# Narrow matrix products of a hybrid decoder step placed on different column tiles, two scan steps at a time

## The chip, the core and the metric

The kernel runs on one core of a Trainium2 chip. A core has five engines with instruction streams of their own: TensorE (PE, matrix products into the PSUM banks), VectorE (DVE), ScalarE (ACT), GpSimd (POOL) and SyncE (SP, which here only issues transfers). Engines wait for each other through semaphores. The metric is the device time of one execution in microseconds, a median over several runs.

## The reference, cut to what matters

One inference step of a decoder layer for 512 prompt tokens and 8 sample tokens. After a projection `z = h @ w_in`, three mixers run: a diagonal complex state-space model (SSM), sparse attention with gates per head, and a short convolution. Their merged output goes through `w_out`, and a mixture of experts follows, whose router chooses a group of experts and two experts in it.

```python
    bu_re = jnp.einsum('blgc,gpc->blgp', ug, bbar_re)
    bu_im = jnp.einsum('blgc,gpc->blgp', ug, bbar_im)
    ...
    _, _, hr, hi = lax.associative_scan(complex_affine_combine, (a_r, a_i, bu_re, bu_im), axis=1)
    y = (jnp.einsum('blgp,gcp->blgc', hr, c_re.astype(f32))
         - jnp.einsum('blgp,gcp->blgc', hi, c_im.astype(f32)))
    y = y.reshape(bsz, seq, SSM_DIM) + d_skip.astype(f32) * u32
    ...
    gates = jax.nn.sigmoid(gate_logits.astype(f32)).reshape(bsz, seq, 3, KV_HEADS, grp)[..., None]
    ...
    lg = (t @ w_rg).astype(f32) + b_rg.astype(f32)
    le = ((t @ w_re).astype(f32) + b_re.astype(f32)).reshape(n_tok, N_EXPERT_GROUPS, EXPERTS_PER_GROUP)
```

## The kernel before

Features lie on the partitions and tokens on the free axis, 520 tokens in two halves of 260 (`CHUNKS`). All data are fp32, and each product written in the code appears in the trace as two passes of the same shape.

The order on every engine is written out by hand. The projection is cut into 22 tiles of 128 columns (`z_tile`, L1527). The SSM has 24 groups, scanned two at a time in 12 steps (`SN`), and the steps are interleaved with the tiles. In step i, TensorE does the tiles `beside[i]` (two in steps 0 to 8, one in step 9, none in 10 and 11), then `bu(i + 1)`, the scan's input products (L1539 for the prompt, L1541 for the samples), then `y(i)`, the outputs (L1551 and L1552, real and imaginary part). The 32 output rows of step i go to partitions 32 * (i % 4) of bank 6, so four steps fill the bank. In step 9 the product of the attention gates (24 outputs, L1612, banks 0 and 1) stands before `bu(10)`; in step 10 the prompt's compression comes before y(10), in step 11 the prompt's scores (L1587) before y(11).

VectorE's step i is a chain: angles and coefficients (L1037 to L1044, with the angles of step i + 1 between them), products with bu (L1050 to L1060; after the first of them TensorE may overwrite bu, `v_done`), two hardware scans (L1063, L1066), four products with cosine and sine into `cgr`, `sgr`, `sgi`, `cgi` (L1070 to L1073), and the states `hr` and `hi` (L1076, L1077), which release y(i) through `h_ready`. One pair of buffers holds the states, so L1076 of step i waits for y(i - 1) (`y_done`). After every fourth step VectorE adds the skip term to bank 6 (L1084) and with this frees the bank (`skip_ready`).

ScalarE copies the projection's tiles out of PSUM and computes sine and cosine. GpSimd does the short convolution (from L589) beside the scan, one block of channels as its tiles become ready, and starts most page loads of the cache. In the attention stage `hidden_part` (L1720) compresses cached blocks with weights of 64 columns, key on column tile 0 and value on column tile 64, in turn.

Late in the kernel the output projection (L1857) makes eight tiles; after each one, `logits(n - 1)` multiplies one block of the normalised tokens with the router's 20 columns (L1846), halves of tokens in banks 6 and 7.

Of the kernel before, what the change touches and what calls it, by code (L numbers as in the profile page):

```python
# [11 lines left out]
ACT = mybir.ActivationFunctionType  # L12
# [4 lines left out]
KD = D // P  # L17
# [133 lines left out]
def build(nc, io):  # L151
    ctx = ExitStack()
    with ctx:
# [82 lines left out]
        def cc(name, rows=P):  # L236
# [165 lines left out]
        hr, hi = WORK[:, 10, :], WORK[:, 11, :]  # L402

        pR, pI, qR, qI, vr, vi, gr, gi, cgr, cgi, sgr, sgi = (
            CMP[:, 1, 2048 + 512 * j:2560 + 512 * j] for j in range(12))
        kint = ki.bitcast(I32)
# [313 lines left out]
        def _(act):  # L720
# [25 lines left out]
            for i in range(SN):  # L746
# [7 lines left out]
                if i == 9:  # L754
                    act.wait_ge(z_done, NZ + 1)
                    for c, (a, b) in enumerate(CHUNKS):
                        mm = act.activation(Gt[:, a:b], bank[c][0:24, 0:HALF], ACT.Sigmoid)
                    mm.then_inc(z_ready, 1)
# [155 lines left out]
            act.activation(lgT[:, HALF:T], bank[7][0:20, 0:HALF], ACT.Copy).then_inc(lt_ready, 1)  # L914
# [49 lines left out]
        def _(dve):  # L964
# [67 lines left out]
            for i in range(SN):  # L1032
# [36 lines left out]

                step(dve.tensor_tensor(cgr, c, gr, ALU.mult), 1)  # L1070
# [3 lines left out]
                if i >= 1:  # L1074
                    dve.wait_ge(y_done, i)
# [437 lines left out]
        def _(pe):  # L1513
# [31 lines left out]
            def y(i):  # L1545

                r = slice(32 * (i % 4), 32 * (i % 4) + 32)
                pe.wait_ge(h_ready, i + 1)
                if i >= 4:
                    pe.wait_ge(skip_ready, i // 4)  # L1550
                pe.matmul(bank[6][r, :], CT[:, i, 0, :], hr, start=True, stop=False, tile_position=(0, r.start))  # L1551
                pe.matmul(bank[6][r, :], CT[:, i, 1, :], hi, start=False, stop=True,  # L1552
                          tile_position=(0, r.start)).then_inc(y_done, 1)
# [49 lines left out]
            for i in range(SN):  # L1603
                for t in beside[i]:
                    z_tile(t)
                if i == 9:

                    pe.wait_ge(wg_in, 16)
                    pe.wait_ge(z_ready, NZ - 1)
                    for k in range(KD):  # L1610
                        for c, (a, b) in enumerate(CHUNKS):
                            mm = pe.matmul(bank[c][0:24, 0:HALF],  # L1612
                                           wgt[:, k, :], H[:, k, a:b], start=(k == 0), stop=(k == KD - 1))
                    mm.then_inc(z_done, 1)
# [6 lines left out]
                y(i)  # L1621
# [220 lines left out]
            def logits(k):  # L1842

                pe.wait_ge(norm_ready, KD + k + 1)
                for c, (lo, hi_) in enumerate(CHUNKS):
                    mm = pe.matmul(bank[6 + c][0:20, 0:HALF], rw[:, k, :], H[:, k, lo:hi_], start=(k == 0),  # L1846
                                   stop=(k == KD - 1))
# [255 lines left out]
```

## Time and profile before

| | |
|---|---|
| three runs, us | 1056.26, 1060.02, 1060.38 (median 1060.02) |
| the profiled execution, us | 1054.12, span 1052.4 |
| mean granted TensorE clock | 0.937 of full speed |
| busy, share of the span | PE 90%, DVE 55%, ACT 25%, POOL 25% |
| chain that ended last | PE 59%, DVE 27%, DMA 5%, issue 5%, ACT 2% |
| L1527 (projection tiles) | 704 passes, 159.4 us busy |
| L1551 and L1552 (y) | 24 passes each, 592 ns and more each by the record |

The profile is one execution. Times in its rows are microseconds from the span's start. A record of a matmul includes its way through the array, and neighbouring records overlap, so the cost of one in a dense stretch is the distance from start to start, which the chain of waits shows directly. The chain follows the work that ended last back from the end: an engine's line in it means that this work set the time there. Idle time in brackets in a timeline names who ended it.

### The profile page before, as it was taken

The page shows a single profiled execution, that of the slowest core. Times are in us where ns is not written, and L with a number is a line of the kernel's source. Part 1 is how long each engine was busy: PE and PEld are TensorE (multiplying, and loading weights), DVE is VectorE, ACT ScalarE, POOL GpSimd, SP SyncE. Part 2 cuts the span into 40 slices and gives each one's busy share as a digit, 9 for nine tenths or more (in the row PEclk, how much of TensorE's full clock was granted, in tenths as well). Part 3 has the DMA queues.
Part 4 walks back from the last instruction along what each step waited for, and adds up shares of the span by engine and source line. Part 5 has one row for each costly group of instructions (what it writes and reads, how often), then busy time and mean ns, then how long its engine had stood idle before and what let it go on. Part 6 is the DMA issues. An engine that isn't in the chain of part 4 may idle for free.

```text
span 1052.4 us, 14165 instructions
## 1 busy us (share of the span) xinstructions
PE 942.6 (90%) x4998; PEld 647.9 (62%) x4998; DVE 581.4 (55%) x982; ACT 258.5 (25%) x569; POOL 261.9 (25%) x285
## 2 busy tenths in 40 slices
PE   4999999998698999899999979989973999999934
PEld 3777776754565666688888858867752333333314
DVE  2697699899655777498999970001135121112125
ACT  3111211222446667322112111211140111111102
POOL 3020065500334541012143512220002122222030
PEclk8999999997799999799999989989995999999967
DMA  8333111110547867114322602381121699999563
GB/s 322 123 98 103 41 61 59 61 62 1 165 139 237 267 207 273 58 56 183 121 76 82 236 32 70 93 360 61 60 68 35 215 337 346 339 333 336 194 164 120
DMA packets 57266, 162.97 MB, mean 155 GB/s; under 512 B 14364, under 2 KB 33325, under 8 KB 51957
## 3 DMA queue, kind: packets, MB, share of 16 engines
q1 hardware_dynamic: 41685, 130.39, 35.4%
q0 software_dynamic: 15520, 31.79, 10.2%
q8 instruction: 36, 0.59, 0.2%
q14 instruction: 25, 0.20, 0.1%
HBM read 197.46 MB, written 18.58 MB: 205 GB/s over the span
## 4 chain that ended last, share of the span: by engine, by line
PE 59%; DVE 27%; DMA 5%; issue 5%; ACT 2%; SPq 2%; POOL 1%; DVEq 0%; POOLq 0%; ACTq 0%
PE bank L1932 11%; PE bank L1527 9%; PE bank L1772 6%; PE bank L1857 6%; PE bank L1958 5%; DVE BIG L1213 5%; PE bank L1720 5%; DVE BIG L1209 3%; PE bank L1781 3%; DMA BIG<-in_w_o 2%; PE bank L1665 2%; DVE BIG L1194 2%; DVE WORK L1195 2%; PE bank L1675 2%; PE bank L1686 1%
## 5 line engine op out<-in xcount | busy, mean ns | idle before, releaser
L1772 PE MATMUL bank<-H,BIG 128*128 128x260 f32 x768 | 175.3, 387 | 1.4 <-ACT AUX L869 1.4
L1527 PE MATMUL bank<-H,BIG 128*128 128x260 f32 x704 | 159.4, 388 | 8.0 <-DVE H L716 8.0
L1772 PEld LDWEIGHTS bank<-H,BIG 128*128 128x128 f32 x768 | 147.2, 192 | 25.6 <-issue 1.8
L1527 PEld LDWEIGHTS bank<-H,BIG 128*128 128x128 f32 x704 | 134.4, 192 | 36.5 <-issue 15.9
L1932 PE MATMUL bank<-BIG,H 128*64 (+1 forms) x512 | 114.8, 601 | 1.9 <-issue 1.9
L434 POOL DMA_DIRECT2D BIG<-in_cmp x128 | 69.8, 546 | 128.4 <-issue 95.8
L1932 PEld LDWEIGHTS bank<-BIG,H 128*64 128x64 f32 x512 | 37.1, 139 | 76.0 <-issue 76.0
L1781 PE MATMUL bank<-BIG 128*128 128x260 f32 x320 | 76.1, 390 | 2.1 <-DVEq L1312 1.3
L1720 PE MATMUL bank<-BIG,AUX 128*64 128x256 f32 x512 | 70.7, 398 | 3.5 <-issue 3.5
L1781 PEld LDWEIGHTS bank<-BIG 128*128 128x128 f32 x320 | 62.0, 194 | 12.4 <-DVEq L1312 1.4
L1857 PE MATMUL bank<-WORK,BIG 128*128 128x260 f32 x256 | 60.1, 394 | 5.2 <-DMA BIG<-in_w_o 5.2
L624 POOL TENSOR_TENSOR AUX<-AUX 128x520 f32<-128x520 f32 x16 | 34.8, 2173 | 113.0 <-ACT AUX L875 113.0
L1475 DVE COPY BIG<-bank 128x256 f32<-128x256 f32 x16 | 6.8, 424 | 98.3 <-PE bank L1943 98.3
L1958 PE MATMUL bank<-BIG 128*64 (+1 forms) x256 | 58.5, 598 | 1.6 <-DVE BIG L1475 1.0
L1857 PEld LDWEIGHTS bank<-WORK,BIG 128*128 128x128 f32 x256 | 49.3, 195 | 15.7 <-issue 8.2
L1213 DVE TENSOR_TENSOR BIG<-BIG 128x2048 f32<-128x2048 f32 (+4 forms) x40 | 51.3, 1282 | 1.4
L869 ACT ACTIVATE AUX<-bank 128x260 f32<-128x260 f32 x48 | 16.0, 385 | 130.5 <-PE bank L1772 130.4
L1327 DVE TENSOR_TENSOR BIG<-BIG,bank 128x260 f32<-128x260 f32 x16 | 6.1, 422 | 73.6 <-PE bank L1857 73.6
L1720 PEld LDWEIGHTS bank<-BIG,AUX 128*64 128x64 f32 x512 | 34.2, 141 | 18.9 <-issue 9.9
L622 POOL TENSOR_TENSOR WORK<-AUX 128x520 f32 x8 | 16.1, 2013 | 106.2 <-ACT AUX L875 106.2
L642 POOL DMA_INDIRECT H<-h_rows,token_i x16 | 15.9, 995 | 103.6 <-DVEq L1455 98.8
L1481 DVE TENSOR_SCALAR WORK<-bank,WORK 128x512 f32<-128x512 f32 x16 | 12.0, 751 | 48.1 <-PE bank L1958 48.1
(411 smaller groups left out, 1378.2 us busy)
## 6 DMA issues: line engine op xcount, KB each, us to landing
BIG<-in_w_gu SPq DMA_DIRECT2D x16, 2048.0 KB, 9.2
BIG<-in_cmp POOLq DMA_DIRECT2D x128, 128.0 KB, 3.5
BIG<-in_cmp SPq DMA_DIRECT2D x128, 128.0 KB, 3.4
BIG<-in_w_d SPq DMA_DIRECT2D x16, 1024.0 KB, 8.7
BIG<-in_w_m SPq DMA_DIRECT2D x24, 512.0 KB, 3.5
BIG<-in_w_z SPq DMA_DIRECT2D x22, 512.0 KB, 3.3
y_rows<-WORK SPq DMA_DIRECT2D x16, 512.0 KB, 9.1
o_win<-BIG SPq DMA_DIRECT2D x2, 2048.0 KB, 9.3
```

Source lines behind the costliest of these rows:

```text
L434: engine.dma_start(CMP[:, b, g * 256:g * 256 + 256], io["cmp"][bass.ds(at, 1)].rearrange("o p n -> p (o n)")).then_inc(arrived, 16)
L624: pool.tensor_tensor(SG[:, b], SG[:, b], BB[:, b], ALU.mult).then_inc(pool_step, 1)
L1194: step(dve.tensor_tensor(P3, KV[br][0], QR[:, m].unsqueeze(1).broadcast_to([P, SELB, HD]), ALU.mult))
L1209: step(dve.tensor_tensor(P3, KV[br][1], SE[:, br, m].unsqueeze(2).broadcast_to([P, SELB, HD]), ALU.mult))
L1213: step(dve.tensor_tensor(P3[:, 0:keys], P3[:, 0:keys], P3[:, keys:2 * keys], ALU.add))
L1527: mm = pe.matmul(bank[2 * (t % 2) + c][:, 0:HALF], W_RING[:, t % 2, k, :], H[:, k, a:b], start=(k == 0), stop=(k == KD - 1))
L1720: mm = pe.matmul(bank[6 + b][v * HD:v * HD + HD, 0:2 * NCB], w1[:, v, r, :], page[b][:, :, v, :, r, :].rearrange("p g h c -> p h g c"), st ...
L1772: mm = pe.matmul(bank[c][:, 0:HALF], W_RING[:, b, k, :], H[:, k, lo:hi_], start=(k == 0), stop=(k == KD - 1))
L1781: mm = pe.matmul(bank[2 + c][:, 0:HALF], WB[:, b, k, :], Z[:, y0 + k, lo:hi_], start=(k == 0), stop=(k == nk - 1))
L1857: mm = pe.matmul(bank[2 * b + c][:, 0:HALF], W_RING[:, b, k, :], M[:, k, lo:hi_], start=(k == 0), stop=(k == KD - 1))
L1932: mm = pe.matmul(bank[2 + i % 2][r, :].rearrange("p (w f) -> p w f", w=2), XT[i % 2][:, k * P + r.start:k * P + r.stop], w[:, :, k, :], st ...
L1958: mm = pe.matmul(bank[5 + half][r, :], ACTT[i % 2][:, f * P + r.start:f * P + r.stop], w[:, f, 512 * half:512 * half + 512], start=(f == 0 ...
```

## The change

Three narrow products are placed on other column tiles of TensorE. The outputs of two scan steps, i and i + 1, are computed together after step i + 1's `bu`, in the order real part of i, real part of i + 1, imaginary part of i, imaginary part of i + 1. For this the states need two pairs of buffers: even steps keep the old one, odd steps write them in place into `cgr` and `sgr`. VectorE therefore waits for the outputs before the four products of an even step and no longer before the states. The gates' and the router's second half of tokens goes to output partitions from 64 instead of 0, and the readers on ScalarE follow.

```diff
@@ build
-        hr, hi = WORK[:, 10, :], WORK[:, 11, :]
...
+        states = ((WORK[:, 10, :], WORK[:, 11, :]), (cgr, sgr))
@@ ScalarE: gates' sigmoid, router's logits to SBUF
-                        mm = act.activation(Gt[:, a:b], bank[c][0:24, 0:HALF], ACT.Sigmoid)
+                        mm = act.activation(Gt[:, a:b], bank[c][64 * c:64 * c + 24, 0:HALF], ACT.Sigmoid)
...
-            act.activation(lgT[:, HALF:T], bank[7][0:20, 0:HALF], ACT.Copy).then_inc(lt_ready, 1)
+            act.activation(lgT[:, HALF:T], bank[7][64:84, 0:HALF], ACT.Copy).then_inc(lt_ready, 1)
@@ VectorE: scan step i
+                if i >= 2 and i % 2 == 0:
+                    dve.wait_ge(y_done, i)
                 step(dve.tensor_tensor(cgr, c, gr, ALU.mult), 1)
                 step(dve.tensor_tensor(sgr, s, gr, ALU.mult), 1)
                 step(dve.tensor_tensor(sgi, s, gi, ALU.mult), 1)
                 step(dve.tensor_tensor(cgi, c, gi, ALU.mult), 1)
-                if i >= 1:
-                    dve.wait_ge(y_done, i)
+                hr, hi = states[i % 2]
                 step(dve.tensor_tensor(hr, cgr, sgi, ALU.subtract), 1)
                 step(dve.tensor_tensor(hi, sgr, cgi, ALU.add))
@@ TensorE: outputs of the scan
-            def y(i):
-
-                r = slice(32 * (i % 4), 32 * (i % 4) + 32)
-                pe.wait_ge(h_ready, i + 1)
+            def y_pair(i):
+
+                pe.wait_ge(h_ready, i + 2)
                 if i >= 4:
                     pe.wait_ge(skip_ready, i // 4)
-                pe.matmul(bank[6][r, :], CT[:, i, 0, :], hr, start=True, stop=False, tile_position=(0, r.start))
-                pe.matmul(bank[6][r, :], CT[:, i, 1, :], hi, start=False, stop=True,
-                          tile_position=(0, r.start)).then_inc(y_done, 1)
+                for part in range(2):
+                    for n in (i, i + 1):
+                        r = slice(32 * (n % 4), 32 * (n % 4) + 32)
+                        mm = pe.matmul(bank[6][r, :], CT[:, n, part, :], states[n % 2][part], start=(part == 0),
+                                       stop=(part == 1), tile_position=(0, r.start))
+                        if part:
+                            mm.then_inc(y_done, 1)
@@ TensorE: gates' product
-                            mm = pe.matmul(bank[c][0:24, 0:HALF],
-                                           wgt[:, k, :], H[:, k, a:b], start=(k == 0), stop=(k == KD - 1))
+                            mm = pe.matmul(bank[c][64 * c:64 * c + 24, 0:HALF], wgt[:, k, :], H[:, k, a:b],
+                                           start=(k == 0), stop=(k == KD - 1), tile_position=(0, 64 * c))
@@ TensorE: loop over scan steps
-                y(i)
+                if i % 2:
+                    y_pair(i - 1)
@@ TensorE: logits
-                    mm = pe.matmul(bank[6 + c][0:20, 0:HALF], rw[:, k, :], H[:, k, lo:hi_], start=(k == 0),
-                                   stop=(k == KD - 1))
+                    mm = pe.matmul(bank[6 + c][64 * c:64 * c + 20, 0:HALF], rw[:, k, :], H[:, k, lo:hi_],
+                                   start=(k == 0), stop=(k == KD - 1), tile_position=(0, 64 * c))
```

On TensorE in the scan, before, from the end of bu(1) (L1541) on: each step has its own y behind bu.

```order
L1541 MATMUL bank<-BIG,TWICE 128x8
L1551 MATMUL bank<-WORK,TWICE 32x512
L1552 MATMUL bank<-WORK,TWICE 32x512
L1527 MATMUL bank<-H,BIG 128x260 x32
L1539 MATMUL bank<-BIG,TWICE 128x512
L1541 MATMUL bank<-BIG,TWICE 128x8
L1539 MATMUL bank<-BIG,TWICE 128x512
L1541 MATMUL bank<-BIG,TWICE 128x8
L1551 MATMUL bank<-WORK,TWICE 32x512
L1552 MATMUL bank<-WORK,TWICE 32x512
L1527 MATMUL bank<-H,BIG 128x260 x32
```

The same place after the change (L1528 is the projection's tile, L1540 and L1542 are bu): from bu(1) through the first pair, L1554.

```order
L1542 MATMUL bank<-BIG,TWICE 128x8
L1528 MATMUL bank<-H,BIG 128x260 x32
L1540 MATMUL bank<-BIG,TWICE 128x512
L1542 MATMUL bank<-BIG,TWICE 128x8
L1540 MATMUL bank<-BIG,TWICE 128x512
L1542 MATMUL bank<-BIG,TWICE 128x8
L1554 MATMUL bank<-WORK,TWICE 32x512
L1554 MATMUL bank<-BIG,TWICE 32x512
L1554 MATMUL bank<-WORK,TWICE 32x512
L1554 MATMUL bank<-BIG,TWICE 32x512
L1528 MATMUL bank<-H,BIG 128x260 x32
L1540 MATMUL bank<-BIG,TWICE 128x512
```

Step 0 has no y left; the y of steps 0 and 1 stand behind bu(2), real and imaginary parts in turn, and read WORK (even step) and BIG (odd step).

On TensorE at the end of the scan, before: the prompt's compression (L1558, L1560), y(10), the scores (L1587), y(11), then transposes.

```order
L1558 MATMUL bank<-w,BIG 16x64 x2
L1560 MATMUL bank<-BIG,w 64x16 x2
L1551 MATMUL bank<-WORK,TWICE 32x512
L1552 MATMUL bank<-WORK,TWICE 32x512
L1587 MATMUL bank<-BIG 128x512 x4
L1551 MATMUL bank<-WORK,TWICE 32x512
L1552 MATMUL bank<-WORK,TWICE 32x512
```

After the change (compression L1562 and L1564, scores L1591):

```order
L1562 MATMUL bank<-w,BIG 16x64 x2
L1564 MATMUL bank<-BIG,w 64x16 x2
L1591 MATMUL bank<-BIG 128x512 x4
L1554 MATMUL bank<-WORK,TWICE 32x512
L1554 MATMUL bank<-BIG,TWICE 32x512
L1554 MATMUL bank<-WORK,TWICE 32x512
L1554 MATMUL bank<-BIG,TWICE 32x512
```

The y of step 10 has left its place before the scores and stands with that of step 11 behind them.

On VectorE in step 2, before, from the second scan (L1066) on; names in brackets are the semaphores waited for:

```order
L1066 SCALAR_TENSOR_TENSOR BIG<-spar,BIG 128x512 [waits dve_step]
L1070 TENSOR_TENSOR BIG<-WORK,BIG 128x512 [waits dve_step]
L1071 TENSOR_TENSOR BIG<-WORK,BIG 128x512 [waits dve_step]
L1072 TENSOR_TENSOR BIG<-WORK,BIG 128x512 [waits dve_step]
L1073 TENSOR_TENSOR BIG<-WORK,BIG 128x512 [waits dve_step]
L1076 TENSOR_TENSOR WORK<-BIG 128x512 [waits y_done,dve_step]
L1077 TENSOR_TENSOR WORK<-BIG 128x512 [waits dve_step]
L1079 COPY hlast<-WORK 128x1 [waits dve_step]
```

The same place after the change, where L1072 to L1075 are the four products and L1077, L1078 the states:

```order
L1066 SCALAR_TENSOR_TENSOR BIG<-spar,BIG 128x512 [waits dve_step]
L1072 TENSOR_TENSOR BIG<-WORK,BIG 128x512 [waits dve_step,y_done]
L1073 TENSOR_TENSOR BIG<-WORK,BIG 128x512 [waits dve_step]
L1074 TENSOR_TENSOR BIG<-WORK,BIG 128x512 [waits dve_step]
L1075 TENSOR_TENSOR BIG<-WORK,BIG 128x512 [waits dve_step]
L1077 TENSOR_TENSOR WORK<-BIG 128x512 [waits dve_step]
L1078 TENSOR_TENSOR WORK<-BIG 128x512 [waits dve_step]
L1080 COPY hlast<-WORK 128x1 [waits dve_step]
```

The wait for `y_done` has moved four products up, to the first of an even step; odd steps have none.

## Rows read from the trace of the kernel before

**Rows 1.** Chain of waits, scan step 1: start us, us, engine, tile, line, count.
```profile
69.28 14.22 PE bank L1527 x64
83.50 1.05 PE bank L1539 x2
...
85.75 0.97 PE bank L1551 x2
86.73 0.86 PE bank L1552 x2
```

**Rows 2.** Timeline of DVE, steps 4 to 8: start us, us, line, out<-in [idle before <-releaser].
```profile
124.33 0.75 DVE L1084 SCALAR_TENSOR_TENSOR BIG<-BIG,sdb,bank 128x512 f32<-128x512 f32 x1 [8.59 <-PE bank L1552]
125.22 0.49 DVE L1037 TENSOR_SCALAR WORK<-WORK,spar 128x512 f32<-128x512 f32 x1
...
140.65 0.90 DVE L1037 TENSOR_SCALAR WORK<-WORK,spar 128x512 f32<-128x512 f32 x1
...
159.82 0.68 DVE L1077 TENSOR_TENSOR WORK<-BIG 128x512 f32<-128x512 f32 x1
...
194.44 0.68 DVE L1077 TENSOR_TENSOR WORK<-BIG 128x512 f32<-128x512 f32 x1
...
200.14 0.75 DVE L1084 SCALAR_TENSOR_TENSOR BIG<-BIG,sdb,bank 128x512 f32<-128x512 f32 x1 [4.53 <-PE bank L1552]
201.03 1.41 DVE L1037 TENSOR_SCALAR WORK<-WORK,spar 128x512 f32<-128x512 f32 x1
```

**Rows 3.** Timeline of PE, bu(6) and y(5).
```profile
158.72 0.28 PE L1541 MATMUL bank<-BIG,TWICE 32*128 32x8 f32 x2
160.61 1.04 PE L1551 MATMUL bank<-WORK,TWICE 128*32 128x512 f32 x2 [1.61 <-DVEq L1078]
```

**Rows 4.** Timeline of PE, end of the scan: y(10), scores, y(11), samples' outputs.
```profile
252.52 1.92 PE L1551 MATMUL bank<-WORK,TWICE 128*32 128x512 f32 x2
...
256.07 4.41 PE L1587 MATMUL bank<-BIG 128*128 128x512 f32 x8
261.45 1.04 PE L1551 MATMUL bank<-WORK,TWICE 128*32 128x512 f32 x2 [0.96 <-DVEq L1078]
262.33 1.02 PE L1552 MATMUL bank<-WORK,TWICE 128*32 128x512 f32 x2
...
268.63 0.88 PE L1639 MATMUL bank<-hlast,TWICE 128*32 128x8 f32 x48 [3.46 <-DVEq L1105]
```

**Rows 5.** Chain of waits, output projection and router.
```profile
707.70 9.13 PE bank L1857 x32
...
724.33 0.98 PE bank L1846 x4
725.32 7.21 PE bank L1857 x32
...
765.31 0.98 PE bank L1846 x4
```

**Rows 6.** Timeline of PE, compression of the cached blocks in the attention stage.
```profile
292.38 1.08 PE L1720 MATMUL bank<-BIG,AUX 128*64 128x256 f32 x8
293.30 0.39 PE L1686 MATMUL bank<-WORK 128*64 128x128 f32 x4
```

**Rows 7.** Windows: stretch, length, PE PEld DVE ACT POOL busy, PEclk, DMA, GB/s.
```profile
160.00:180.00 20.00, 18.57 (x77) 13.83 (x78) 19.63 (x28) 2.56 (x7) 11.31 (x10) 1.00 0.17 53
266.00:268.00 2.00, 0.00 (x0) 0.00 (x0) 1.76 (x8) 0.00 (x0) 0.00 (x0) 0.95 0.00 0
268.00:270.00 2.00, 0.88 (x48) 0.81 (x48) 0.80 (x4) 0.00 (x0) 0.50 (x1) 0.50 0.06 11
```

**Rows 8.** Timeline of GpSimd (POOL), third channel block of the convolution.
```profile
192.42 3.84 POOL L589 TENSOR_TENSOR rstd<-BIG 128x520 f32<-128x520 f32 x1 [20.32 <-ACT BIG L728]
```

**Rows 9.** Timeline of PE, the gates' product.
```profile
227.48 7.19 PE L1612 MATMUL bank<-H,wgt 128*24 128x260 f32 x32
```

**Rows 10.** Timeline of DVE, first use of bu(10).
```profile
238.12 0.68 DVE L1050 TENSOR_TENSOR BIG<-WORK,bank 128x512 f32<-128x512 f32 x1
```

## The prediction

> **What bounds the kernel now.** I read the chain of waits through the scan stage first, since most of the diff lies there, then the timelines of TensorE (PE) and VectorE (DVE) where the chain changes engine. In a step with two projection tiles the chain runs on PE alone: 64 passes of the tiles in 14.22 us, two input products (`bu`), then `y` in 0.97 + 0.86 = 1.83 us, and the next tiles at once [rows 1]. The reader should see that nothing lies between these pieces: PE is full, and a microsecond off `y` is a microsecond off the step. DVE meanwhile is done early and waits: 8.59 us before the skip-add of step 3 and 4.53 before that of step 7 [rows 2]. After each skip-add the roles change: steps 4 to 6 and 8 to 11 run at DVE's pace, a step from 125.22 to 140.65 being 15.4 us, and PE waits for h, 1.61 us before y(5) [rows 3], 0.96 before y(11) [rows 4]. So PE time is worth something in steps 0 to 3 and 7, and little elsewhere until step 11, where y(11) is on the path alone. In the output projection (L1857) the chain is PE again: 7.21 us a tile and 0.98 for the router's four passes between two tiles [rows 5].
>
> **What a pair costs.** Every fp32 product is two passes: a 260-column one takes 14.22/64 = 0.222 us, a 512-column one about 0.43 (0.86 for L1552's two) [rows 1]. The trace has no pair of 32-column tiles side by side. It has the like: L1720 alternates two 64-column tiles, two passes on each, and eight passes of 256 columns take 1.08 us, the next line starting after 0.92 [rows 6]. One after the other they would take 8 x 0.219 = 1.75 us (0.222 scaled to 256 columns). Five times 0.219 is 1.09: the second pass of one tile runs beside the first of the other, so eight passes fill five slots. The new pair has the same order (two passes on tile n, two on n+1, and again). I price it at 5 x 0.43 + 0.11 = 2.26 us, the 0.11 being what the first half of y takes over two slots (0.97 - 0.86). Bounds: four slots (1.83) if all overlapped, eight (3.55) if nothing did. The Trainium skill (TensorE: Matmul & The Clock Gate, Part 3: Packing small matmuls) has a rule against this: weight loads overlap matmuls in flight only when the row groups differ, and all tiles here use all rows. By that rule the pair would take the upper bound and no edit here would gain; the 1.08 us of [rows 6], on tiles that share all rows too, disagrees with it.
>
> **Steps 0 to 3.** Four y of 1.83 go (7.32), two pairs come (4.52): the skip-add of step 3 starts 2.8 us earlier, at 121.5 instead of 124.33 [rows 2].
>
> **Steps 4 to 7.** DVE waits for nothing in them and moves with the skip-add, so h(5) is ready at 160.50 - 2.8 = 157.7 and h(7) at 195.12 - 2.8 = 192.3 [rows 2]. PE ends bu(6) at 159.00 [rows 3]; now 2.8 earlier and without y(4), at 154.4. It then waits 3.4 us for h(5): the wait of 1.61 grows, since the pair needs the odd step's h and PE has less to do before it. The pair ends at 160.0. Two rounds of tiles and bu follow, 16.47 each (69.28 to 85.75, [rows 1]), now without y(6) between them; PE reaches the next pair at 192.9, 0.6 after h(7), and ends it at 195.2. The skip-add of step 7 starts at 195.3 against 200.14: 4.8 earlier. PE and DVE meet there almost together, so nothing more is to be had from PE, and any delay of PE after step 5 is paid in full.
>
> **The clock in the new wait.** That delay is likely. Through today's waits of up to 1.61 us the granted clock stays 1.00 (160 to 180 us); in the 3.46 us before the product at 268.63 it falls, 0.95 in 266 to 268 and 0.50 (the 1.2 GHz level) after [rows 4, 7]. The new 3.4 us is as long as that one. A restart at the low level costs what the first output tile after the idle stretch shows: 9.13 us against 7.21, 1.9 us [rows 5]. Bounds are 0 (the clock holds) and 1.9; I take 1.9. What is late next is the pair of steps 6 and 7, and with it the skip-add: 2.9 earlier instead of 4.8.
>
> **GpSimd beside DVE.** GpSimd starts its third convolution at 192.42 [rows 8], and DVE's first operation of step 8 takes 1.41 us where that of step 4 took 0.49 [rows 2]. DVE's idle time from h(7) to the skip-add hides part of this. It was 5.0 us; with the fall of the clock it is still about 4.9 and nothing changes, without it 3.0, and I charge 0.6 (bounds 0 and two operations longer by 0.92).
>
> **Steps 8 to 11.** DVE sets the pace and waits for no product, so y(8), y(9) and the gates' product leave covered time. The gates' 32 passes (7.1 us from 227.48, [rows 9]) become 17 slots, 3.8 us; bu(10) after them is used by DVE at 238.12, without a wait, right behind its own work [rows 10]. Worth 0; without DVE's cover it would be 3.3. The last pair takes the place of y(11): 2.26 against 1.90 (261.45 to 263.35, [rows 4]), about +0.35, if the clock is high. Today y(10) (1.92 for two passes, low clock) and the scores stand before it and bring the clock up, and y(11) starts after 0.96 us idle at full speed [rows 4]. Now y(10) moves into the pair, the scores come sooner, and the waits before h(9) and bu(11) grow by about 2 to 4 us. At the low clock the pair takes 5 x 0.96 = 4.8, +2.9. Between 0.35 and 2.9 I take 1.0, nearer the low end since eight dense passes of the scores still run shortly before it.
>
> **DVE's own edits** cost nothing: the same count of operations of the same shapes, odd steps writing in place. The wait for y_done moves from the end of every step to the four products of even ones. Behind it stand those products and h; the pair it waits for runs right after the bu that the same step uses, and between that use and the four products DVE has ten operations, two of them scans. If it were not, its delay would go into every second step.
>
> **Router.** The logits were already 32-column work at (0,0); moving the second half to column 64 makes 3 slots of 4 passes: 0.22 us a visit. Six of the eight visits lie before the last output tile's end [rows 5]: -1.3. The other two lie beside ScalarE's work, 0. Bounds: 0 and -1.8.
>
> **Sum.** -4.8 + 1.9 + 0 + 1.0 - 1.3 = -3.2 us. The profiled execution took 1054.12 us (span 1052.4), 5.9 under the median of the three runs, 1060.02. I make the forecast against that median: 1056.8; a profiled execution like the one shown would take 1050.9.
>
> **Rivals.**
> 1. The clock holds through the new wait. For it: bu before and the pair after are dense. Against: the 3.46 us row. -4.8 + 0.6 + 0.35 - 1.3 = -5.2, 1054.8.
> 2. A cold tail: the longer waits of steps 9 and 10 leave the clock low until the last pair. For it: the tail is at the low level already when y(10) runs. Against: the scores lie before the pair. The tail term is 2.9 instead of 1.0: 1058.7.
> 3. The other side, and the change not doing what it says: 32-column tiles do not run side by side. With p for a pair, the skip-add of step 7 moves by 4p - 13.9 (two pairs in steps 0 to 3, one in 5, one in 7) and the tail by p - 1.9: 5p - 15.8, zero at p = 3.15, about seven slots of eight. At eight, p = 3.55 gives +1.9 and the router 0: 1061.9, and 1063.8 with the clock's fall. For it: no row shows 32-column tiles at once. Against: the 64-column row. The Trainium skill's rule above would lead here.
>
> **How the numbers follow.** Forecast 0.45, rival 1 0.25, rival 2 0.15, rival 3 0.10, others 0.05. Predicted is the likeliest, 1056.8. The runs shown spread over 4.1 us, so each case carries about 2 us either way; 1052.5 to 1061 takes in the first three and leaves out most of rival 3 and the lower edge of rival 1. Half a per cent, 5.3 us, is about what a measurement can tell from no change. Under 1054.7 lie nearly half of rival 1, a sixth of the forecast and some of the others: 0.27. Over 1065.3 lie only rival 3 with the clock and stray cases: 0.05. Within: 0.68.
>
> **What would show it.** In the changed kernel's timeline: a pair group of eight passes lasting near 2.2 us (3.5 refutes the pricing); skip-adds near 121.5 and 195 to 197; PE idle 3 to 4 us before the pair of steps 4 and 5, with the granted clock at 0.5 there or 1.0 (decides rival 1); the gates' group near 3.8 us with no change in DVE; router visits near 0.76 us. Wrong would be the prediction if DVE waited at its new wait, if the scan's end moved by under 1 or over 6 us, or if time moved after the scan other than at the router.

## The result, and the profile after the change

| | before | after |
|---|---|---|
| median of four runs each, us | 1058.37 (1056.26 to 1060.38) | 1045.72 (1044.50 to 1046.84) |
| ratio, 95% interval | | 0.9883 [0.9854, 0.9913] |
| profiled execution, us (span) | 1054.12 (1052.4) | 1046.84 (1045.2) |
| mean granted TensorE clock | 0.937 | 0.930 |

The change is faster, by more than the forecast and outside its range (1052.5 to 1061). The two profiled executions differ by 7.3 us, the medians by 12.65; that the two numbers differ is itself a finding, taken up below.

In the changed kernel L1528 is the projection's tile, L1540 and L1542 are bu, L1554 is the pair, L1616 the gates, L1591 the scores, L1862 the output projection, L1851 the router, L1085 VectorE's skip-add. The chain of waits through the scan, from bu(2) and the first pair on (start, length, what), answers to [rows 1]:

```profile
81.15 1.05 PE bank L1540 x2
...
83.40 1.84 PE bank L1554 x8
85.24 14.22 PE bank L1528 x64
```

Eight passes of 512 columns take 1.84 us where a single y of four passes took 1.83 [rows 1]. The second state's output is free. The timeline of TensorE shows how, and then the places where the engine waited. A row here is one pass or a run of alike passes, with its start and length; the time in brackets is the wait before it.

```profile
83.33 0.62 PE L1554 MATMUL bank<-WORK,TWICE 128*32 128x512 f32 x1
83.34 0.62 PE L1554 MATMUL bank<-BIG,TWICE 128*32 128x512 f32 x1
83.79 0.59 PE L1554 MATMUL bank<-WORK,TWICE 128*32 128x512 f32 x1
83.79 0.59 PE L1554 MATMUL bank<-BIG,TWICE 128*32 128x512 f32 x1
...
156.45 1.06 PE L1554 MATMUL bank<-WORK,TWICE 128*32 128x512 f32 x1 [3.46 <-DVEq L1079]
...
157.31 1.06 PE L1554 MATMUL bank<-WORK,TWICE 128*32 128x512 f32 x1
...
160.01 14.88 PE L1528 MATMUL bank<-H,BIG 128*128 128x260 f32 x64
...
229.08 1.06 PE L1554 MATMUL bank<-WORK,TWICE 128*32 128x512 f32 x1 [4.05 <-DVEq L1079]
...
236.26 2.02 PE L1540 MATMUL bank<-BIG,TWICE 32*128 32x512 f32 x2 [3.55 <-DVEq L1057]
...
251.19 6.48 PE L1591 MATMUL bank<-BIG 128*128 128x512 f32 x8 [0.84 <-ACT vcp L774]
257.60 0.62 PE L1554 MATMUL bank<-WORK,TWICE 128*32 128x512 f32 x1
```

Read the starts: a pass of the even step (WORK) and one of the odd step (BIG) begin within 0.01 us of each other, and the next two 0.43 us later. So four slots, not five. At 156.45 TensorE has waited 3.46 us, and the passes on one tile now start some 0.85 us apart (157.31) where it was 0.43: the new wait costs the clock, as forecast. The waits ahead of 229.08 and 236.26 are as long, and the work after them is slow too, but the last pair at 257.60 is at full speed. The granted clock (PEclk, the third value from the end) in windows of that stretch, to be held against [rows 7]:

```profile
154.00:156.00 2.00, 0.00 (x0) 0.00 (x0) 2.00 (x4) 0.00 (x0) 1.80 (x3) 0.60 0.00 0
156.00:160.00 4.00, 3.55 (x8) 0.56 (x8) 3.78 (x8) 0.00 (x0) 3.81 (x3) 0.50 0.02 4
160.00:162.00 2.00, 2.00 (x8) 1.71 (x7) 2.00 (x4) 0.00 (x0) 1.92 (x2) 0.69 0.00 0
162.00:164.00 2.00, 2.00 (x11) 1.71 (x10) 2.00 (x5) 0.00 (x0) 1.90 (x2) 1.00 0.00 0
```

VectorE's skip-adds of steps 3, 7 and 11 (start, length, and in brackets its wait), which answer to [rows 2]:

```profile
120.19 0.75 DVE L1085 SCALAR_TENSOR_TENSOR BIG<-BIG,sdb,bank 128x512 f32<-128x512 f32 x1 [6.80 <-PE bank L1554]
...
195.62 0.75 DVE L1085 SCALAR_TENSOR_TENSOR BIG<-BIG,sdb,bank 128x512 f32<-128x512 f32 x1 [4.94 <-PE bank L1554]
...
259.66 0.75 DVE L1085 SCALAR_TENSOR_TENSOR BIG<-BIG,sdb,bank 128x512 f32<-128x512 f32 x1 [2.62 <-PE bank L1554]
```

The third stands in the trace of before at:

```profile
263.46 0.75 DVE L1084 SCALAR_TENSOR_TENSOR BIG<-BIG,sdb,bank 128x512 f32<-128x512 f32 x1 [1.64 <-PE bank L1552]
```

They come 4.1, 4.5 and 3.8 us earlier. The scan hands on 3.8 us. Most of the rest comes from the router, in the chain of waits through the output projection, where a visit takes 0.55 us against 0.98 in [rows 5]:

```profile
720.12 0.55 PE bank L1851 x4
720.67 7.21 PE bank L1862 x32
...
758.93 0.55 PE bank L1851 x4
```

Six such visits lie on the chain, 0.43 us each: 2.6 us. The first tile of the output projection starts 4.3 us earlier (703.41 against 707.70), the end of that stage comes 6.8 us earlier (766.7 against 773.5), the end of the span 7.2.

### The profile page after: what moved, and what is told of

Read it like the earlier page. It is cut to its first block, busy times and chain, and to the rows that moved or that the text cites. A ratio compares the mean times of both kernels' runs of the same rounds, so it can differ in the third digit from the quotient of the medians.

```text
span 1045.2 us, 14150 instructions
## 1 busy us (share of the span) xinstructions
PE 930.3 (89%) x4998; PEld 644.6 (62%) x4998; DVE 580.0 (55%) x982; ACT 258.5 (25%) x569; POOL 267.5 (26%) x285
## 4 chain that ended last, share of the span: by engine, by line
PE 62%; DVE 24%; DMA 5%; issue 4%; ACT 2%; SPq 2%; POOL 1%; DVEq 0%; POOLq 0%; ACTq 0%
PE bank L1937 11%; PE bank L1528 10%; PE bank L1777 6%; PE bank L1862 6%; PE bank L1963 5%; DVE BIG L1214 5%; PE bank L1725 5%; DVE BIG L1210 3%; PE bank L1786 3%; DMA BIG<-in_w_o 2%; PE bank L1670 2%; PE bank L1540 2%; DVE BIG L1195 2%; DVE WORK L1196 2%; PE bank L1680 2%
## 5 line engine op out<-in xcount | busy, mean ns | idle before, releaser
L1528 PE MATMUL bank<-H,BIG 128*128 128x260 f32 x704 | 159.8, 388 | 7.8 <-DVE H L716 7.8
L1528 PEld LDWEIGHTS bank<-H,BIG 128*128 128x128 f32 x704 | 134.7, 193 | 33.1 <-issue 12.4
L1862 PE MATMUL bank<-WORK,BIG 128*128 128x260 f32 x256 | 60.2, 395 | 5.1 <-DMA BIG<-in_w_o 5.1
L1862 PEld LDWEIGHTS bank<-WORK,BIG 128*128 128x128 f32 x256 | 49.4, 195 | 15.7 <-issue 8.1
L622 POOL TENSOR_TENSOR WORK<-AUX 128x520 f32 x8 | 18.8, 2354 | 103.3 <-ACT AUX L875 103.3
```

Source lines behind the costliest of these rows:

```text
L1528: mm = pe.matmul(bank[2 * (t % 2) + c][:, 0:HALF], W_RING[:, t % 2, k, :], H[:, k, a:b], start=(k == 0), stop=(k == KD - 1))
L1862: mm = pe.matmul(bank[2 * b + c][:, 0:HALF], W_RING[:, b, k, :], M[:, k, lo:hi_], start=(k == 0), stop=(k == KD - 1))
```

## The experiments

Twelve kernels ran in three sets, each set beside the kernel before on the same chip. Ratios are to the kernel before of the same set, with 95% intervals.

**Both kernels again, and the change in parts.** The kernel before and the changed kernel unchanged; then only the pairs (the gates' and the router's second half back at partition 0); then only the router; in the second set only the gates. ScalarE's readers of the moved halves follow and are left out below, as is the edit of the pairs alone.

```diff
 only the router:
-                    mm = pe.matmul(bank[6 + c][0:20, 0:HALF], rw[:, k, :], H[:, k, lo:hi_], start=(k == 0),
-                                   stop=(k == KD - 1))
+                    mm = pe.matmul(bank[6 + c][64 * c:64 * c + 20, 0:HALF], rw[:, k, :], H[:, k, lo:hi_],
+                                   start=(k == 0), stop=(k == KD - 1), tile_position=(0, 64 * c))
 only the gates:
-                            mm = pe.matmul(bank[c][0:24, 0:HALF],
-                                           wgt[:, k, :], H[:, k, a:b], start=(k == 0), stop=(k == KD - 1))
+                            mm = pe.matmul(bank[c][64 * c:64 * c + 24, 0:HALF], wgt[:, k, :], H[:, k, a:b],
+                                           start=(k == 0), stop=(k == KD - 1), tile_position=(0, 64 * c))
```

> The kernel before, unchanged. The two profiled executions differ by 7.3 us (1054.12 and 1046.84), the medians by 12.65. Theory 'spread': the profiled pair shows the whole effect and the executions of the kernel before merely vary by several us; then this one against itself gives a ratio of 1.000, and executions between 1053 and 1061. Theory 'hidden': another 5 us of the effect is real and not in the profiled pair; then nearly all executions here lie above 1056.

> The changed kernel, unchanged, on the same chip as the kernel before. Theory 'spread': ratio near 0.993 (7 us). Theory 'hidden': ratio near 0.988 (12 us). In its profile again: pairs of 1.84 us at full clock, the pair of steps 4 and 5 at the low clock (3.6 us), skip-adds near 120.2, 195.6 and 259.7 us.

> Only the pairs of the scan, gates and router as before. By the chains of the two profiles the scan's end moves by 3.8 to 4.1 us and the router by 2.6; theory 'all on the chain': this one gives 4 us (ratio 0.996) and the output loop keeps 0.98 us per visit of the router. Rival: the gates' product has a part in the scan's gain; then under 3 us here.

> Only the router's second half of tokens on column tile 64, scan and gates as before. Theory 'pairs of passes fill half the slots': a visit takes 0.55 us instead of 0.98, six of them on the chain, 2.6 us (ratio 0.9975). Theory of the prediction (three slots of four): 0.76 us a visit, 1.3 us.

> The kernel before with one part of the change alone: the gates' two halves of tokens side by side on column tiles 0 and 64. Theory A (the gates' 3.5 us of TensorE are hidden behind VectorE's states of steps 10 and 11): gates 3.7 us instead of 7.2, skip-adds within 0.5 us of those of the kernel before, ratio within 0.3% of 1. Theory B (the change's gain that the profiled executions did not show, 1058.4 against 1045.7 in the medians with 7.3 us in the profiles, comes from the gates): 3 us or more faster.

| kernel | median, us | range | ratio |
|---|---|---|---|
| before again | 1057.14 | 1052.03 to 1063.17 | 0.9993 [0.9968, 1.0019] |
| changed again | 1047.16 | 1046.15 to 1049.27 | 0.9900 [0.9866, 0.9934] |
| pairs only | 1052.31 | 1047.26 to 1057.89 | 0.9956 [0.9932, 0.9980] |
| router only | 1050.70 | 1048.29 to 1057.39 | 0.9938 [0.9914, 0.9962] |
| gates only | 1056.91 | 1053.93 to 1065.40 | 0.9999 [0.9973, 1.0024] |

Against the 1056.52 of the kernel before in the first set the pairs bring 4.2 us and the router 5.8, together 10.0; the whole change brought 9.4 there. The parts add up as far as the intervals tell (some 2.6 us to either side), and the gates bring nothing. Of the theories on the two kernels, the kernel before against itself gives 0.9993, as 'spread' had it; the changed kernel's 0.9900 lies between the two forecasts, 0.993 and 0.988, and its interval holds both.

The router alone brought more than either theory of its run allowed. A visit takes 0.55 us on its chain, as the first theory said, and six of them are worth 2.6 us; the median fell by 5.8. What the rest can be is taken up at the end of the account below.

In the timeline of TensorE with the gates alone the reason shows:

```profile
231.18 3.69 PE L1612 MATMUL bank<-H,wgt 128*24 128x260 f32 x32
...
243.09 2.07 PE L1539 MATMUL bank<-BIG,TWICE 32*128 32x512 f32 x2 [4.13 <-DVEq L1057]
```

The product takes 3.69 us instead of 7.19 [rows 9], and what it saves is waited out ahead of the next input product, which waits 4.13 us for VectorE and then runs at the low clock. Its skip-adds of steps 7 and 11 (201.90 and 266.75) are not within 0.5 us of those in the first trace of before, as was expected, but 1.8 and 3.3 us later, where the second trace of before has them (201.95 and 266.81).

The run of the kernel before shows something that its first profile did not. Its span is 1058.8, and these are rows of its timeline of TensorE in the scan (y of steps 6 and 8):

```profile
180.13 1.92 PE L1551 MATMUL bank<-WORK,TWICE 128*32 128x512 f32 x2 [0.80 <-DVEq L1078]
...
220.46 1.71 PE L1551 MATMUL bank<-WORK,TWICE 128*32 128x512 f32 x2 [2.15 <-DVEq L1078]
```

and of its chain behind the output projection:

```profile
779.27 2.51 PE bank L1870 x20
781.77 1.85 PE bank L1846 x4
783.62 1.88 PE bank L1880 x8
```

A record of two passes at full speed is 1.04 or 1.02 us [rows 4] and a visit of the router 0.98 [rows 5]: here the same instructions run at the low clock (granted 0.60 from 180 to 184, where the first profile has 1.00). The waits ahead of them are 0.80 and 2.15 us in the scan and 0.70 in the tail; in the first profile they were 0.81, 1.94 and 0.70, and the clock stayed up. The scan ends 3.3 us later, 0.3 of it there already at step 3, and from the end of the output projection (777.6) to the router's ranks (L1894, 795.7) it takes 18.1 us instead of 15.7.

**Is it the overlap?** The outputs of the two steps are issued one after the other instead of in turn, first freely, then with a wait on the first step's own end between them.

```diff
 in series:
-                for part in range(2):
-                    for n in (i, i + 1):
+                for n in (i, i + 1):
+                    for part in range(2):
 apart, in addition:
+                    if n > i:
+                        pe.wait_ge(y_done, n)
```

> The changed kernel with the two loops of a pair swapped: all four passes of the first step's state go out before the four of the second, instead of one part of each in turn. Nothing else differs; the outputs still stand on two column tiles and are still computed after the second state. Theory A (the pair takes 1.84 us because passes on the two column tiles run at the same time, and it is the issue in turn that brings them together): the pair takes eight slots, 3.4 to 3.7 us, the skip-add behind steps 6 and 7 moves from 195.6 to 198 or later, and the time is 4 to 5 us above the changed kernel's, about 1051. Theory B (what gains is only that the first step's output is put off beyond the second state, so that it no longer stands ahead of it): the pair's length matters little, the skip-add stays within 1 us of 195.6 and the time within 2 us of 1046.

> The changed kernel with the pair's second output held back until TensorE has finished the first: the four passes of the first step go out, then a wait on their own end, then the four of the second. The outputs still stand on two column tiles and behind the second state; only the overlap is gone. Theory A (the gain of the scan is the overlap, eight passes in 1.84 us): a pair takes 3.6 to 4.2 us, the skip-add behind steps 2 and 3 comes at 123.8 to 125, that is where the kernel before has it (124.33) and 4 us behind the changed kernel's 120.19, and the time is 5 us or more above the changed kernel's, near that of the kernel with the router's part alone (about 1051). Theory B (the gain is that the first output no longer stands ahead of the second step's input product): the skip-add stays at 122 or earlier and the time within 2.5 us of 1046.

In series, free: 1046.19 us, 0.9897 [0.9865, 0.9930], no different from the changed kernel's 0.9900. Its timeline of TensorE, with the first and second pass in order of time and what follows the pair:

```profile
83.26 0.62 PE L1554 MATMUL bank<-WORK,TWICE 128*32 128x512 f32 x1
83.27 0.62 PE L1554 MATMUL bank<-BIG,TWICE 128*32 128x512 f32 x1
...
85.10 5.09 PE L1528 MATMUL bank<-H,BIG 128*128 128x260 f32 x22
```

The order of issue in the code is WORK four times, BIG four times, and still the first pass on BIG begins 0.01 us after the first on WORK, and the next tile 1.84 us after the pair's start. So half of theory A, that the issue in turn brings the passes together, is wrong: the engine finds them itself. This kernel therefore did not tell overlap from deferral, which is why the second one was made. Apart: 1056.08 us, 1.0003 [0.9980, 1.0027]. Its timeline of TensorE:

```profile
83.43 1.90 PE L1556 MATMUL bank<-WORK,TWICE 128*32 128x512 f32 x4
85.39 1.90 PE L1556 MATMUL bank<-BIG,TWICE 128*32 128x512 f32 x4
87.22 3.12 PE L1528 MATMUL bank<-H,BIG 128*128 128x260 f32 x13
...
160.43 3.62 PE L1556 MATMUL bank<-WORK,TWICE 128*32 128x512 f32 x4 [3.43 <-DVEq L1079]
164.11 2.56 PE L1556 MATMUL bank<-BIG,TWICE 128*32 128x512 f32 x4
```

and VectorE's skip-adds of steps 3 and 7:

```profile
124.16 0.75 DVE L1085 SCALAR_TENSOR_TENSOR BIG<-BIG,sdb,bank 128x512 f32<-128x512 f32 x1 [8.72 <-PE bank L1556]
...
203.53 0.75 DVE L1085 SCALAR_TENSOR_TENSOR BIG<-BIG,sdb,bank 128x512 f32<-128x512 f32 x1 [8.72 <-PE bank L1556]
```

A pair takes 3.79 us (83.43 to 87.22). The skip-add of step 3 is back where the kernel before has it (124.33), that of step 7 comes 3.4 us later than there, and the router's gain is used up. Deferral without overlap is a loss, because the new wait and its low clock come with it; all of the scan's gain is the overlap. The loss is larger than this run's forecast had it (about 1051 us): the pairs of steps 8 and 9 and of 10 and 11 wait and lose the clock too, and the skip-add of step 11 (269.22) comes 5.8 us later than in the kernel before.

**The clock in the new wait.** Four full-width products that nobody reads, ahead of the pair of steps 4 and 5 in the changed kernel.

```diff
             def y_pair(i):
+                if i == 4:
+                    pe.wait_ge(skip_ready, 1)
+                    for _ in range(4):
+                        pe.matmul(bank[6][:, :], ones[:], H[:, 0, 0:512], start=True, stop=True)
                 pe.wait_ge(h_ready, i + 2)
```

> The changed kernel with four full-width fp32 products that nobody reads ahead of the pair of steps 4 and 5, where TensorE otherwise waits 3.5 us for the second state. Theory A (the granted clock falls for want of work in that wait, and the pair and the input product behind it pay 1.8 and 0.6 us for it): the clock stays at 1.00 from 152 to 164, the pair takes 1.84 us there, the skip-add of steps 6 and 7 comes 2.4 us earlier, near 193.2, and the time falls by about 2.4 us against the changed kernel. Theory B (the low clock there costs nothing at the end, since VectorE's next states set the pace): the clock stays up but the skip-add and the time do not move by more than 0.5 us.

1043.83 us, 0.9877 [0.9846, 0.9908]. The medians of this set put it 2.4 us under the pairs in series, whose work is the changed kernel's; the intervals overlap, so the verdict rests on the trace. Its timeline of TensorE:

```profile
152.81 3.70 PE L1551 MATMUL bank<-H,ones 128*128 128x512 f32 x8
156.44 0.62 PE L1558 MATMUL bank<-WORK,TWICE 128*32 128x512 f32 x1
...
158.28 14.29 PE L1528 MATMUL bank<-H,BIG 128*128 128x260 f32 x64
```

and its skip-add of step 7:

```profile
193.30 0.75 DVE L1085 SCALAR_TENSOR_TENSOR BIG<-BIG,sdb,bank 128x512 f32<-128x512 f32 x1 [2.73 <-PE bank L1558]
```

The granted clock is 1.00 from 152 to 164. The pair starts when it did (156.44) and the next tiles 1.7 us sooner; these save another 0.6 (14.29 against 14.88). The skip-add is 2.3 us earlier than the changed kernel's 195.62. Theory A holds, with 2.3 us where 2.4 were forecast.

**Is the rest of the gain the clock in the kernel before?** The kernel before with one filling product in the router's tail, then also with fillings in the scan.

```diff
 tail, ahead of L1870:
+            pe.matmul(bank[3][:, 0:260], ones[:], M[:, 0, 0:260], start=True, stop=True)
 scan, in y(i), in the second kernel alone:
+                if i in (5, 6, 8):
+                    pe.wait_ge(skip_ready, i // 4)
+                    for _ in range({5: 3, 6: 1, 8: 4}[i]):
+                        pe.matmul(bank[6][r, 0:260], ones[:, 0:32], H[:, 0, 0:260], start=True, stop=True,
+                                  tile_position=(0, r.start))
```

> The kernel before with one product of 260 columns that nobody reads, ahead of the twenty products with one column that follow the output projection's last visit of the router. Theory A (in most executions of the kernel before the granted clock falls in the router's tail, and that is 2.4 us of the gain that the first profiled execution did not show): 15.7 us from the end of the output projection to the router's ranks (L1894 of the kernel before), the clock held there, and a median 1 to 2.4 us below that of the kernel before. Theory B (the tail's 18.1 us come from something else, an engine or a transfer): 18.1 us in the profile all the same and no lower median.

> The same, and in the scan of the kernel before three, one and four narrow products of 260 columns that nobody reads, in the waits ahead of the outputs of steps 5, 6 and 8. Theory A (the executions of the kernel before differ by where the clock falls in the scan and in the router's tail, and the two together are the 5 us by which the medians differ more than the two profiled executions): outputs of steps 6 and 8 at full clock (1.9 us each), the gated unit starts at 270 to 271 and not at 274, and the median is 3 to 5 us below that of the kernel before, 1052 to 1053.5, with runs closer together. Theory B: the outputs stay at full clock but the median is within 1.5 us of the kernel before, so that the 5 us have another cause.

Tail alone: 1056.03 us (1051.01 to 1063.84), 0.9981 [0.9957, 1.0005]. The filling did not hold the clock in the profiled execution, the longest of the twelve (1063.84), as its timeline of TensorE shows (the filling, then the router's last visit):

```profile
778.09 0.71 PE L1867 MATMUL bank<-WORK,ones 128*128 128x260 f32 x2 [0.61 <-DVEq L1331]
...
780.84 1.92 PE L1846 MATMUL bank<-H,rw 128*20 128x260 f32 x4
```

From the end of the output projection (776.5) to the ranks (795.0) it is 18.5 us. So theory A's filling failed here, and since the clock was low all the same, the run does not tell the two theories apart. With the scan filled as well: 1053.24 us (1051.62 to 1059.45), 0.9961 [0.9938, 0.9983]. In its timeline of TensorE the same filling stands ahead of a visit at full speed, and the output of step 6 is slow although the wait ahead of it was filled to 0.26 us:

```profile
179.15 1.91 PE L1556 MATMUL bank<-WORK,TWICE 128*32 128x512 f32 x2 [0.26 <-DVEq L1078]
...
775.02 0.71 PE L1872 MATMUL bank<-WORK,ones 128*128 128x260 f32 x2 [0.60 <-DVEq L1331]
...
777.40 1.05 PE L1851 MATMUL bank<-H,rw 128*20 128x260 f32 x4
```

The median, 3.4 us below that of the kernel before, and the narrower range are what theory A expected, the mechanism in single places is not: these fillings did not decide whether the clock fell there. What decides stays open.

**A version faster than both.** The changed kernel with fillings in five waits, and a second time with those ahead of the output projection moved.

```diff
 both, fill(bank, source, n) being n products as above: in y_pair(i)
+                if i in (4, 8):
+                    pe.wait_ge(skip_ready, i // 4)
+                    fill(6, H[:, 0, 0:512], 4)
 ahead of the samples' outputs and the gated unit behind the scan
+            fill(6, H[:, 0, 0:512], 4)
 ahead of the first hidden parts
+            fill(5, H[:, 0, 0:512], 2)
 first kernel, ahead of the output projection:
             pe.wait_ge(mm_ready, 26)
             pe.wait_ge(mb_ready, 25)
+            fill(4, H[:, 0, 0:512], 5)
 second kernel:
+            fill(4, H[:, 0, 0:512], 4)
             pe.wait_ge(mm_ready, 26)
             pe.wait_ge(mb_ready, 25)
```

> The changed kernel with products that nobody reads in five waits of TensorE: four full-width ones ahead of the pairs of steps 4/5 and of steps 8/9, four ahead of the gated unit behind the scan, two ahead of the hidden parts of the attention and five ahead of the first tile of the output projection. Theory A (these waits are where the clock falls, and each first group behind them pays for it): 2.4 us at steps 4/5, about 1 at steps 8/9, 1.9 at the gated unit (9.9 to 8.0 us), up to 1.9 at the hidden parts and 1.9 at the first projection tile (9.2 to 7.2): 7 to 9 us below the changed kernel, 1037 to 1040. Theory B (what is late there is set by VectorE, ScalarE or a transfer): groups get shorter but begin no earlier behind, under 3 us in all.

> The changed kernel with the products that nobody reads as in the run with five fillings, but those ahead of the first tile of the output projection (four of them now) put ahead of the wait for the merged blocks, not behind it, where they held the tile up. Theory A (there, too, the clock falls for want of work, and the loss of that run was the place alone): the first tile starts at 696 to 697 instead of 701.9 and takes 7.2 us, everything behind it comes 5 us earlier, 1037 to 1040. Theory B (the tile's start is set by the transfer of its weights, which comes no earlier): it starts at 700 or later, and the time stays within 2 us of 1044.5.

The first: 1044.54 us, 0.9879 [0.9849, 0.9909], no better than with the one filling (1043.83). From its timeline of TensorE:

```profile
264.40 8.16 PE L1664 MATMUL bank<-BIG,TWICE 128*128 128x260 f32 x36 [1.15 <-ACT BIG L782]
...
279.16 1.08 PE L1734 MATMUL bank<-BIG,AUX 128*64 128x256 f32 x8
...
694.77 7.25 PE L1548 MATMUL bank<-H,ones 128*128 128x512 f32 x10 [3.58 <-POOL WORK L626]
701.86 7.18 PE L1872 MATMUL bank<-WORK,BIG 128*128 128x260 f32 x32
```

The gated unit takes 8.16 us (9.93 in the changed kernel), the first hidden parts 1.08 (1.98). But the last filling starts only after the wait for GpSimd, at 694.77, runs at the low clock itself (7.25 us for ten passes) and holds the projection until 701.86. Moved ahead of the wait, from the timeline of TensorE of the second:

```profile
234.45 2.07 PE L1540 MATMUL bank<-BIG,TWICE 32*128 32x512 f32 x2 [5.27 <-DVEq L1057]
...
690.82 3.60 PE L1548 MATMUL bank<-H,ones 128*128 128x512 f32 x8
695.76 7.25 PE L1872 MATMUL bank<-WORK,BIG 128*128 128x260 f32 x32 [1.34 <-DMA BIG<-in_w_o]
...
761.22 1.78 PE L1895 MATMUL bank<-cst,H 128*104 128x128 f32 x8
```

1039.38 us (1036.95 to 1041.20), 0.9837 [0.9813, 0.9861]: theory A, and no run of it is as long as the shortest of the changed kernel (1044.50). The changed kernel did not run in this set; the kernel before has medians of 1056.5, 1056.5 and 1056.7 in the three. The first projection tile starts 7.6 us earlier than in the changed kernel and takes 7.25 instead of 9.21. Not every filling paid: the one ahead of the pair of steps 8 and 9 holds the clock there, but the next input product then waits 5.27 us for VectorE and runs at the low clock as before (2.07 us, the first row). The last row, eight passes that take 1.08 us in the changed kernel, shows that the new tail can lose its clock too: 16.6 us from the end of the projection to the ranks here, 15.7 in the changed kernel.

## Why the prediction was wrong, step by step

**The price of a pair: the failed step.** The forecast took 2.26 us, five slots, from the 64-column tiles of [rows 6]. That group's record lasts 1.08 us, but the next line starts 0.92 after it, and a record includes the way through the array. By start to start, the measure that the text used everywhere else, 0.92 / 0.219 is four slots. Five came from the record's end, which overlaps the next group. Measured: 1.84. The 0.96 us for a slot at the low clock was a record's too (1.92 for two passes [rows 4]); by starts it is 0.85. The forecast's own formula for the skip-add of step 7, 4p - 13.9, gives -6.5 with p = 1.84; where the filling held the clock, -6.8 was measured (193.30 against 200.14). With the 2.3 us of the clock it gives -4.2; measured -4.5. With p = 3.79 of the pairs kept apart it gives +1.3, with the 2.4 us that the slow pair lost there +3.6; measured +3.4. So all three were measured 0.2 to 0.3 us earlier than the formula has them. That much, and a little more, was gained ahead of the first pair and not by the change: bu(2) starts at 81.15 instead of 83.50 [rows 1], 2.35 earlier, of which the missing y(0) explains 1.83. In the six traces with the old scan the skip-add of step 3 lies anywhere from 123.64 to 124.67, so this is within what executions differ by. The chain of reasoning around the price stood; only the price was wrong, and at 5p in the scan and a slot a visit at the router it makes up 3.4 of the 4.1 us by which the profiled pair beat the sum.

**The rule weighed there.** The Trainium skill (TensorE: Matmul & The Clock Gate, Part 3: Packing small matmuls) lets weight loads overlap only between different row groups. The tiles here share all rows and run side by side nonetheless, eight passes in 1.84 us against 3.79 kept apart. In the changed kernel's trace the weight load of the first pass on BIG starts at 83.34, with the first pass on WORK (83.33 to 83.95) in flight. The same section's measure of a pack, one matmul and some 4 ns for each further tile, fits starts 0.01 us apart and a pair that takes 1.84 us against 1.83 of one y.

**Rival 3**, no overlap, is refuted; the kernel with the pairs apart shows what it would have been in the scan.

**Steps 0 to 3**: -4.1 instead of -2.8. At the measured price it would be -3.6 (two pairs of 1.84 for four y of 1.83), and 0.5 is the earlier start.

**The clock in the new wait**: right in place and kind, 2.3 us (1.7 at the pair, 0.6 at the tiles) instead of 1.9. Rival 1 is out: the clock fell, and where it was held the skip-add came 2.3 us earlier.

**GpSimd beside VectorE**: 0, as forecast. The third convolution moved with the tiles, from 192.42 to 187.49, and VectorE's first operation of step 8 took 0.98 us instead of 1.41.

**Steps 8 to 11**: +0.7 from skip-add to skip-add (4.5 to 3.8) instead of +1.0. Of the two waits forecast before the last pair both came, with the low clock, and the scores took 6.48 us instead of 4.41 [rows 4]; but they brought the clock up in time, so rival 2's cold pair did not come.

**Gates and VectorE's edits**: 0, as forecast.

**Router**: 0.43 us a visit instead of 0.22, the same error of a slot; -2.6 instead of -1.3.

In the profiled pair: -4.5 + 0.7 - 2.6, and -0.9 in small pieces elsewhere that the forecast put at nothing and no run explains, is -7.3 where -3.2 was forecast. The median missed by 11.1 us (1056.8 to 1045.72): 4.1 in this sum, 1.65 because a fourth run of the kernel before took its median from 1060.02 to 1058.37, and 5.35 by which the medians differ more than the profiled pair.

**The other missing term: the execution that the sum was made on.** The forecast said that its profiled execution lay 5.9 us under the median, and carried the difference over unchanged. That holds only if what made it shorter is untouched by the change. In the three sets the kernel before ran 75 times, from 1052.0 to 1065.5 us, median 1056.5. Sorted by the mean granted clock that each run reports, the 45 runs at 0.933 and more have a median of 1055.8 us, the 30 below it 1060.5. The profiled execution of before, at 0.937 and 1054.1 us, has a clock that one of the 75 reached, and six of them were as short. The second trace of before shows where the clock can go: outputs of the scan (the 3.3 us above, less the 0.3 at step 3) and the router's tail (2.4 us), both places that the change touches. Of the six profiles with the old router's halves (two of them with fillings) the tail's clock fell in four, of the eight with the new halves in one, late, for 0.9 us. The changed kernel's 16 runs (its own, and those with the pairs in series) stay within 1044.2 to 1050.0. So the medians differ by some 10 us over the sets, 7.3 of it visible in the profiled pair; the rest is most likely the old kernel's losses that its profile did not show, and the first measurement's 12.65 rested on four runs a kernel. The same would explain why the router alone brought 5.8 us: its trace keeps the clock in the tail. That the new order is less exposed is an observation from eight and six profiles; the fillings that should have shown it by force did not settle it, so the cause of these last 3 us stays open.

## What to carry to other kernels

Price side-by-side products from start to start, never from a record's end, and try the overlap itself before pricing it in slots: with two narrow fp32 outputs on different column tiles the second one was free. When a change takes dense work off an engine, look for the wait that it opens, since the work behind that wait can run at the low clock; products that nobody reads, issued ahead of the wait and no longer than it, gave back 2.3 us in one place and some 7 in five together, of which one brought next to nothing because the next wait grew. Before a sum made on one profiled execution is carried to a median, ask what differs between executions and whether the change touches it.

## What was not expected of the hardware

Passes on two column tiles paired up in both orders of issue tried: with four on one tile issued ahead of four on the other, the fifth issued begins 0.01 us after the first, and all eight take 1.84 us. The Trainium skill (TensorE: Matmul & The Clock Gate, Part 3: Packing small matmuls) has products start and end in the order of the program; the starts in these records disagree, and so does the group's 1.84 us: in that order the last of the eight could begin only in the seventh slot.

The granted clock falls in some executions and not in others at the same place of the same kernel: y(6) behind a wait of 0.80 us ran at the low level in one trace of before, and behind 0.81 us at the full one in the first (0.60 and 1.00 granted from 180 to 184). What decides was not found.
